# Expert rows moved as quarter rows and turned in 32x32 blocks on VectorE, in a mixture-of-experts encoder block

## What is computed

```python
cap = CAPACITY_FACTOR * n // N_EXPERTS              # 128 prompt rows, 32 sample rows
aff = jax.nn.softmax(xt @ w_router, axis=-1)
gates, idx = lax.top_k(aff.T, cap)
def expert(args):
    idx_e, g_e, wg, wu, wd = args
    xe = xt[idx_e]
    he = jax.nn.silu(xe @ wg) * (xe @ wu)           # 1024 -> 2816
    return (he @ wd) * g_e[:, None]                 # 2816 -> 1024
out = zeros_like(xt).at[idx].add(ye)
```

## Time and profile before

| | |
|---|---|
| median of three runs | 2693.3 us (2691.65 to 2697.71) |
| profiled execution, first to last instruction | 2693.8 us |
| TensorE busy | 2606.6 us (97%) |
| VectorE busy | 1963.9 us (73%) |
| ScalarE busy | 1692.7 us (63%) |
| GpSimd busy | 1108.9 us (41%) |
| mean granted TensorE clock | 0.988 of full |

### The profile page before, as it was taken

How to read it: one execution, slowest core, us unless ns; L and a number is a source line. 1 busy time by engine, 2 the same in 40 slices (tenths; PEclk the granted TensorE clock), 3 DMA queues, 4 the chain that set the end, 5 groups by cost and what they waited for, 6 DMA issues and landing times. The chain is left out here.

```text
span 2693.8 us, 53857 instructions
## 1 busy us (share of the span) xinstructions
PE 2606.6 (97%) x22588; PEld 2372.4 (88%) x22588; DVE 1963.9 (73%) x2361; ACT 1692.7 (63%) x2527; POOL 1108.9 (41%) x781
## 2 busy tenths in 40 slices
PE   7999999989959999999999999999999999999997
PEld 6666776665549999999999999999999999999997
DVE  6233256674668788888878888787878878788787
ACT  4366345562127676676767677676766767677675
POOL 2224201134125364452736346263644627354354
PEclk9999999999969999999999999999999999999998
DMA  7311312124557898979889897988988798898887
GB/s 188 76 46 32 74 37 44 36 85 150 168 199 274 314 313 297 330 256 342 293 319 315 292 333 258 340 294 314 322 293 322 269 330 304 311 323 289 317 299 285
DMA packets 365898, 652.18 MB, mean 242 GB/s; under 512 B 26599, under 2 KB 94055, under 8 KB 365623
## 3 DMA queue, kind: packets, MB, share of 16 engines
q1 hardware_dynamic: 349483, 605.63, 64.5%
q0 software_dynamic: 16176, 43.12, 6.3%
HBM read 612.81 MB, written 36.94 MB: 241 GB/s over the span
## 5 line engine op out<-in xcount | busy, mean ns | idle before, releaser
L1986 DVE TENSOR_TENSOR wl<-stg,wh 128x2048 bf16<-128x2048 f32 (+1 forms) x544 | 1241.0, 2289 | 256.6 <-ACT wh L1476 251.8
L1476 ACT ACTIVATE wh<-stg 128x2048 fp32r<-128x2048 f32 (+1 forms) x544 | 1010.9, 1861 | 196.2 <-PE S L1104 71.4
L2379 POOL TENSOR_TENSOR hx<-hh,hx 128x320 fp32r<-128x320 f32 x176 | 385.6, 2191 | 805.9 <-ACT hx L1529 805.6
L1101 PE MATMUL S<-X,wh 128*128 128x320 f32 x3760 | 591.0, 312 | 1.3 <-DVE X L1995 1.3
L1101 PEld LDWEIGHTS S<-X,wh 128*128 128x128 f32 x3760 | 557.1, 189 | 1.7 <-DVE X L1995 1.7
L1147 PE MATMUL S<-hx,wh 128*128 128x320 f32 x1892 | 312.6, 313 | 0.5 <-DVE yTs L2034 0.5
L1101 PE MATMUL OG<-X,wh 128*128 128x320 f32 x1872 | 298.2, 311 | 1.2 <-DVE gg L2016 1.2
L1104 PE MATMUL S<-Xb,wl 128*128 128x160 bf16 x3760 | 290.1, 233 | 0.0
L1147 PEld LDWEIGHTS S<-hx,wh 128*128 128x128 f32 x1892 | 280.8, 188 | 0.9 <-issue 0.6
L1101 PEld LDWEIGHTS OG<-X,wh 128*128 128x128 f32 x1872 | 277.4, 188 | 1.6 <-issue 1.4
L1104 PEld LDWEIGHTS S<-Xb,wl 128*128 128x128 bf16 x3760 | 258.9, 98 | 12.0
(11 more groups left out here) (316 smaller groups left out, 3803.5 us busy)
## 6 DMA issues: line engine op xcount, KB each, us to landing
stg<-in_w_gate_dram SPq DMA_DIRECT2D x80, 2048.0 KB
stg<-in_w_up_dram SPq DMA_DIRECT2D x80, 2048.0 KB
stg<-in_w_down_dram SPq DMA_DIRECT2D x64, 2048.0 KB
stg<-in_w_down_dram SPq DMA_DIRECT2D x32, 1536.0 KB
stg<-in_w_gate_dram SPq DMA_DIRECT2D x16, 1024.0 KB
stg<-in_w_up_dram SPq DMA_DIRECT2D x16, 1024.0 KB
w_st<-in_w_in_dram SPq DMA_DIRECT2D x20, 512.0 KB, 4.0
yt<-mixed SPq DMA_DIRECT2D x10, 512.0 KB, 5.4
```

Source lines behind the costliest of these rows:

```text
L1101: pe.matmul(out, w, x, start=first, stop=False, skip_group_check=True)
L1476: act.activation(piece_conv(wh, g), piece_stage(g), ACT.Copy).then_inc(rounded, 1)
L1986: dve.tensor_tensor(piece_conv(wl, g), piece_stage(g), piece_conv(wh, g).bitcast(F32), ALU.subtract).then_inc(split, 1)
L2379: pool.tensor_tensor(hx[:, f, CT:2 * CT], hh[:, :, :], hx[:, f, 0:CT].bitcast(F32), ALU.subtract).then_inc(hidden_ready, 1)
```

## The change

The 1024 columns of `ffn_in` and `residual` are stored in another order (column 128 k + m at place 8 m + k), so that a quarter row of 1 KB holds all eight column blocks for 32 values of m. An expert's rows move as five lots (`NB`) of 128 quarter rows: four lots of 32 prompt rows (`SB`) and one of the sample rows; `QD` is 4, `QW` 32. VectorE then turns 32x32 blocks in SBUF, one instruction for x (`x_flip`, 128x5x8x32), two for y (`y_flip`, 128x5x4x32). TensorE's turns go, except for the first expert's x and the last expert's y. ScalarE and VectorE round and split x from `xf` in two instructions each. ScalarE scales y in five (`y_scale`). Each partition must now know the row numbers of its quarter: `index_list` is followed by `index_blocks` on VectorE, a small matmul `index_spread` on TensorE and `index_sum` on VectorE. The core of the diff:

```diff
             def index_list(n):
                 pe.wait_ge(onehot_ready, n)
-                if n >= 3:
-                    pe.wait_ge(y_copied, 4 * (n - 2))
+                if n >= 2:
+                    pe.wait_ge(idx_ready, n - 1)
...
+            def index_spread(n):
+                pe.wait_ge(spread_ready, n)
+                pe.matmul(PT[:, 0, 16:16 + SB * PARTS], same_place[:, :, :].rearrange("p a j -> p (a j)"),
+                          spread[:, :, :].rearrange("p b n -> p (b n)"), start=True, stop=True).then_inc(spread_ps, 1)
...
-                    if k == 1 and e:
-                        for q in (2, 3):
-                            pe.wait_ge(ysum_ready, (e - 1) * KT + 2 * q + 2)
-                            pe.wait_ge(y_copied, 4 * (e - 1) + q - 1)
-                            y_turn(e - 1, q)
                     if k == 9 and e + 1 < NE:
                         index_list(e + 2)
-                    if k == GU and e + 1 < NE:
-                        pe.wait_ge(gathered, (e + 2) * 16)
-                        pe.wait_ge(gathered_s, (e + 2) * 32)
-                        next_x_turn(e, 0)
-                        next_x_turn(e, 1)
-                    if k == GU + 3 and e + 1 < NE:
-                        next_x_turn(e, 2)
-                        next_x_turn(e, 3)
+                    if k == 11 and e + 1 < NE:
+                        index_spread(e + 2)
...
+            def y_scale(e):
+                act.wait_ge(y_flipped, 2 * e + 2)
+                for b in range(NB):
+                    act.activation(yq[:, b, :], yq[:, b, :], ACT.Copy, scale=gate[:, e % 2, b:b + 1]).then_inc(y_scaled, 1)
...
+            def index_blocks(n):
+                dve.wait_ge(idx_ps, n)
+                if n >= 2:
+                    dve.wait_ge(spread_ps, n - 1)
+                dve.tensor_tensor(spread[:, :, :], PT[:, 0, 0:PARTS].unsqueeze(1).to_broadcast([P, SB, PARTS]),
+                                  own_block[:, :].unsqueeze(2).to_broadcast([P, SB, PARTS]), ALU.mult
+                                  ).then_inc(spread_ready, 1)
...
+            def x_flip(e):
+                dve.wait_ge(gathered, gathered_by(e))
+                if e >= 2:
+                    dve.wait_ge(x_split, x_steps(e - 1))
+                b0 = 0 if e else SB
+                dve.transpose(xf[:, :, QW * b0:CT].rearrange("p k (b i) -> p b k i", i=QW),
+                              xg[:, b0:NB, :].rearrange("p b (j k) -> p b k j", j=QW)).then_inc(x_flipped, 1)
...
+            def y_flip(e, half_):
+                dve.wait_ge(ysum_ready, KT * e + 4 * half_ + 4)
+                if e and half_ == 0:
+                    dve.wait_ge(scattered, 16 * NB * e)
+                dve.transpose(yq[:, :, :].rearrange("p b (j k) -> p b k j", j=QW)[:, :, 4 * half_:4 * half_ + 4, :],
+                              yT[:, :, :].rearrange("p c (b i) -> p b c i", i=QW)).then_inc(y_flipped, 1)
...
                     if k == 10 and e + 1 < NE:
+                        if e + 2 == NE:
+                            index_rows(NE)
+                        index_blocks(e + 2)
+                    if k == 12 and e + 1 < NE:
                         index_sum(e + 2)
-                    if k == GU + 2 and e + 1 < NE:
-                        x_lows(4 * (e + 1) + 1, 0, 0)
-                        x_lows(4 * (e + 1) + 2, 1, 1)
-                    if k == GU + 5 and e + 1 < NE:
-                        x_lows(4 * (e + 1) + 3, 2, 0)
-                        x_lows(4 * (e + 1) + 4, 3, 1)
+                    if k == GU - 1 and e + 1 < NE:
+                        x_flip(e + 1)
+                    if k == GU + 3 and e + 1 < NE:
+                        x_lows(e + 1, 0)
+                        x_lows(e + 1, 1)
...
             def scatter(e):
-                pool.wait_ge(y_copied, 4 * e + 4)
+                pool.wait_ge(y_scaled, NB * (e + 1))
...
+                for b in range(NB):
+                    pool.indirect_dma_start(acc_parts, bass.IndirectOffsetOnAxis(ap=idx[:, e % 2, b:b + 1], axis=0),
+                                            yq[:, b, :], None, compute_op=ALU.add).then_inc(scattered, 16)
...
                     if b == 1 and e:
                         scatter(e - 1)
-                    if b == 5 and e + 1 < NE:
+                    if b == 6 and e + 1 < NE:
                         gather(e + 2)
```

More of the change, by code:

```diff
@@ L174 @@
 PARTS = 5
+QD, QW = 4, 32
+SB = CP // QW
+NB = SB + 1
+XCOLS = D // QD
 ROUNDS_AHEAD = {6: (0, 5, 6), 7: (0, 11, 12), 10: (1, 5, 6)}
@@ L371, in build @@
     iotaS = after("iotaS", [P, P], F32)
-    idx = after("idx", [P, 2, 3], U32)
-    gate = after("gate", [P, 2, 2], F32)
+    idx = after("idx", [P, 2, NB], U32)
+    gate = after("gate", [P, 2, NB], F32)
+    row_idx = after("row_idx", [P, 2], U32)
+    row_gate = after("row_gate", [P, 1], F32)
     oh = after("oh", [P, TPR, P], BF16)
@@ L1020, in _ @@
                     for c in range(2):
-                        turn(wo_fill["h", t - 1] + c, [h2t[:, b * P:(b + 1) * P] for b in range(4 * c, 4 * c + 4)])
+                        turn(wo_fill["h", t - 1] + c, [natural(h2t[:, :])[:, b] for b in range(4 * c, 4 * c + 4)])
                 if t >= 2:
@@ L1878, in _ @@
                         dve.wait_ge(h2_ready, u)
-                    own(dve.tensor_tensor(x2t[:, :], S[:, u % 2, :], xt[:, u % 2, :], ALU.add))
+                    own(dve.tensor_tensor(natural(x2t[:, :]), by_block(S[:, u % 2, :]), by_block(xt[:, u % 2, :]), ALU.add))
                     own.wait()
@@ L2272, in list_constants @@
                               allow_small_or_imprecise_dtypes=True))
-                for c in range(4):
-                    for m in range(2):
-                        own.wait()
-                        own(pool.memset(chunk[CS * c:CS * c + CS, m:m + 1], float(4 * m + c)))
+                own(pool.memset(own_block[:, :], 0.0))
+                by_quad = identf[:, :].rearrange("p (a j) -> p a j", a=QD)
+                own(pool.tensor_tensor(col_sums[:, :, :], by_quad[:, 0:2, :], by_quad[:, 2:4, :], ALU.add))
@@ L2277, in list_constants @@
+                for c in range(QD):
+                    own.wait()
+                    own(pool.memset(quad[QW * c:QW * c + QW, :], float(c)))
+                    own(pool.memset(own_block[QW * c:QW * c + QW, c:c + 1], 1.0))
+                own.wait()
+                own(pool.tensor_tensor(same_place[:, :, :], col_sums[:, 0, :].unsqueeze(1).to_broadcast([P, QD, QW]),
+                                       col_sums[:, 1, :].unsqueeze(1).to_broadcast([P, QD, QW]), ALU.add))
                 own.wait()
@@ L2349, in _ @@
-            gather(1)
+                pool.tensor_copy(Xb[:, 4 * m:4 * m + 4, :],
+                                 X[:, 4 * m:4 * m + 4, 0:CT].bitcast(F32)).then_inc(x_b, 1)
+            first_gather()
             pool.sem_inc(gather_sent, 1)
-            for q in range(4):
-                x_bf16(q + 1, q)
+            for m in range(2):
+                x_bf16(0, m)
             def scatter(e):
-                pool.wait_ge(y_copied, 4 * e + 4)
+                pool.wait_ge(y_scaled, NB * (e + 1))
@@ L2390, in _ @@
                 if e + 1 < NE:
-                    for q in range(4):
-                        x_bf16(e * 4 + (4 + q + 1), q)
+                    for m in range(2):
+                        x_bf16(e + 1, m)
             for g in range(2, len(FIN_GROUPS)):
```

317 lines of the change are left out of this document (164 added, 153 removed).

## The result

The changed kernel takes 2771.6 us (median of four runs, 2770.8 to 2772.4), the kernel before 2693.6 in runs beside it: a ratio of 1.0283, with an interval of 1.0271 to 1.0295. It is slower, as forecast, but by 78 us and not by the 43 predicted, and outside the range. The profiled execution spans 2769.8 us against 2693.8, so 76.0 us are to be found.

What follows compares the result with a forecast made beforehand. TensorE, busy 97% of the span, was taken as the bound. With 30.0 and 2 us off and 64.4, 3.3 and 7.5 on, the forecast was 43.2 us longer, 2736.5 us, range 2673 to 2757.

Steps and rivals of the forecast that it cites:

- turns removed: On TensorE, fifteen experts lose two turn groups each of x and y: 30.0 us off.
- piece 11, fifteen experts: TensorE waits for gate sum gg, late because two further scatters hold GpSimd: 3.3 us per expert.
- piece 12, beyond piece 11: TensorE waits for the spread matmul's input in fourteen experts; whole loss there 4.6 us, including 3.3 at piece 11.
- gathers: Three become five on GpSimd, one pair later; hh some 2.2 us late, 0.5 us lost in each of fifteen experts: 7.5.
- start: First turn needs only the first gather, no longer the third: 0 to 4 us less, 2 taken.
- steps of 32 bytes, in the front: Residual and its norm (x2t, h2t) written with a step of 32 bytes: counted as nothing.
- the first half of the scatters' step: Five scatters on GpSimd's queue delay hh and gg, so TensorE's piece 11 waits 3.3 us.
- S: Time the two further scatters add on GpSimd's queue: 3.6 us, between 2.5 and 3.9.
- The index step: VectorE's index_blocks comes too late for TensorE's piece 12: 1.0 us even with the scatters as they are, shifted fully by scatter delay.
- Strides: Writing the residual and its norm in 32-byte steps was counted as free, as they already go one element at a time.
- The rival: x2t and h2t doubled by 32-byte steps, all on the path: 25 us more, 2761 us; chance 0.08.
- VectorE's own work: x_flip 1.4 us and each y_flip 0.7, beside 20.45 us idle: counted nothing, high end a few tenths per expert.

Runs made afterwards that it cites:

- the version with the findings together: Changed kernel with scatters at several places, ffn norm weights reordered once, last expert's sums in natural order, second half of x_lows at k = 28: 2682.9 us.
- the version with spread scatters: Changed kernel with each expert's five scatters issued two behind pair 1 and one each behind pairs 2, 3 and 4, rings of three: 2699.6 us.
- The early list: Changed kernel with its index list made two pieces earlier, on TensorE after piece 7 and on VectorE at k = 8: 2772.7 us.
- the kernel without a spread matmul: Kernel before the change with only two more scatters of zeros per expert, to a table nobody reads, behind its three: 2764.8 us.
- the version with four scatters: Changed kernel with four of the five scatters behind pair 1 and the fifth behind pair 2, rings of three: 2737.7 us.
- the dense front: Changed kernel with the front's x2t and h2t written and read in dense column order, leaving out the columns' reordering: 2754.7 us.

## Why the prediction was right in its sign and wrong in its size

By the prediction's own steps, measured between the starts of the same pieces in the two profiled executions:

| step | predicted, us | measured, us |
|---|---|---|
| turns removed | -30.0 | -32.4 |
| piece 11, fifteen experts | 15 x 3.3 = 49.5 | 53.4 |
| piece 12, beyond piece 11 | 14 x 1.3 = 18.2 | 26.2 |
| gathers | +7.5 | 0 |
| sums of the down stage | 0 | +9.5 |
| start | -2 | -3.9 |
| steps of 32 bytes, in the front | 0 | +16.9 |
| the end, behind the last expert's piece 21 | 0 | +8.3 |

The left column sums to 43.2, the right to 78.0; the 2.0 us above the 76.0 of the spans are the last expert's piece 17, which comes 1.4 us earlier behind its piece 16 than before, and the first expert's start, 0.6 us shorter. (The turns are read from the version with the findings together, in which TensorE doesn't wait at these places: from piece 1 to 2, and from piece 21 to the next expert's first piece, it takes 32.4 us less than the kernel before, 0.51 and mostly 1.62 an expert. In the changed kernel the same two stretches take 22.9 us less, so the sums of the down stage cost 9.5. The front's two lines are good to some microseconds only: with the same front, the first piece starts at 806.48 in the changed kernel's profiled execution and at 800.96 in that of the version with spread scatters, which with 2694.0 us is the fastest of its ten.)

*The turns* were costed nearly rightly, and so was *the first half of the scatters' step*, size and path: S is 3.70 for the assumed 3.6, hh waits 5.78 for 5 to 6, piece 11 waits 3.39 for 3.3, and it waits for gg. The rule of the Trainium skill that it set against the rows ("SBUF — State Buffer", section "Who interferes with whom"), by which wl would not hold an indirect DMA, is again not borne out: the scatter at 1317.69 is held 3.04 us, those that meet no wl take 1.55.

*The index step* was too small and wrong in its reason. S + 1.0 = 4.6 us at piece 12 was meant as a wait for the spread matmul. That wait exists, 0.8 us, and where the clock holds the step comes out as forecast (1.2 us beyond piece 11 for 1.3), but in the changed kernel only in three experts. In the twelve others the slower clock behind the 3.4 us of standing takes its place and costs more, up to 2.7 us. The early list changed nothing, the kernel without a spread matmul has the loss too, the last expert loses 2.6 us there without one, and in the version with four scatters, where the clock holds, the wait for spread is there in all fourteen experts that make a list. The sum for a stall was made with the stall alone; what TensorE does in the microseconds behind it was not in it.

*Strides* are the step that failed outright: "The residual and its norm are written with a step of 32 bytes; I count nothing for now." x2t went from 1225 to 2127 ns and h2t from 1285 to 2065, 10 x (0.90 + 0.78) = 16.8 us, and the dense front takes 16.9 off, so all of it is on the path; the 13.1 us ahead of the first expert are these less the 3.9 that the start gained. The argument against, that they already go one element at a time, did not hold: 1.2 ns an element became 2.0. The rival named 25 us with a chance of 0.08. Its rule, from the Trainium skill ("SBUF — State Buffer", section "Door 1: The DMA port swizzle": lines of 16 bytes, and a penalty for each access that goes to another line), agrees with the rows in kind; it gives no figure, and the rows give 0.8 to 0.9 ns an element, for the one step of 32 bytes that was run. And the prediction went through the places where the strides are written, not through those where they are read: at the end ten norms take 2.20 in place of 1.30 us, four of them in a row ahead of the last rows' sums. That has no term at all. The two together are 25 of the 33 us that were missing.

*Gathers.* The second wait of hh came, 1.45 us in each of fifteen experts for the 2.2 expected; it stays under the margin of 1.74, and no piece from 13 to 21 loses anything. *VectorE's own work* was counted as nothing, with a few tenths per expert as the high end; it cost 0.6. The transposes take 2.62 and 1.46 us, near the doubled bound, and the two halves of x_lows, before apart at k = 24 and 27, now stand together at k = 25. From x_flip to the sums yT, 1373.34 to 1392.35 in the fifth expert, VectorE has no gap left, so whatever is added there pushes the sums. The version with half of x_lows moved behind them lost that wait; how much of it x_flip makes by itself was not run.

*Luck.* That the fifth expert takes 120.91 us for the 120.8 forecast is luck in part: the slower clock stands in for the wait for spread, and the sums for the gathers. The fourteen experts like it take 120.6 to 122.2.

## What to carry to other kernels

Count the instructions that a change adds to an in-order queue against the slack of the next one in it, and place them by that: the same five scatters cost 72 us more at one place than at four. Price a stall of TensorE with the matmuls that follow it, since the clock may fall behind it (here 1.5 to 2.7 us on top of 3.4). Where the profile names what ended a wait, check by the order of the queues that it is the instruction waited for. When a table's order is changed, list every instruction that writes or reads it, and time each access pattern, to the last one of the kernel.

## What the runs showed of the hardware

* Behind a wait of 3.4 us TensorE's next 16 matmuls of 320 columns took 3.4 to 4.6 us instead of 2.5 to 2.6 in 12 of 15 experts of the changed kernel, and 3.3 to 4.1 in 13 of 15 of the kernel with two more scatters, at a mean granted clock of 0.61 to 0.76 over the piece; behind 1.55 us, in fourteen experts, they took 2.58, and in the one behind 1.84 us 4.05. Why equal waits went either way in these experts is open.
* A VectorE operation on float32 in steps of 32 bytes takes 2.0 to 2.2 ns a column, dense 1.2 to 1.3, and it makes little difference whether only the output has the step (x2t) or only one input (the last norms). ScalarE's square of 512 columns of xe takes 0.63 us dense (the kernel before) and 1.13 strided (the changed kernel).
* A 32x32-block transpose of float32 on VectorE takes 2.0 ns a column with one side strided by 32 bytes (2618 ns for 1280), and 2.3 for 640 (1455 ns); no dense one was run.
